# Hybrid FoX / RWKV-7 / retention decoder step: FoX q, k and v projections issued in thirds between the steps of four small stages

## The reference

```
h = rms_norm(x, ln_mix_g);  p = h @ w_in          # 1024 -> FoX q,k,v (512 each), 8 forget, RWKV 896, retention q,k,v,g (256 each)
FoX (8 heads of 64): q,k = rms_norm per head; logf = log_sigmoid(f + b); c = cumsum(logf)
     softmax(q k^T / 8 + c_i - c_j) v, causal; sample tokens also attend 8 cached pages of 128 rows
RWKV-7 (4 heads): S = S*w_t + (S a_t) b_t + v_t k_t; y = S r_t; head norm; bonus; gate
retention (4 heads): q,k = rotary; chunks of 128: o = ((q k^T) * dmask) v + (q R) * cross; R = R*gamma + k^T v; head norm; silu gate
x += [FoX | RWKV | retention] @ w_out
x += (silu(rms_norm(x) @ w_gate) * (rms_norm(x) @ w_up)) @ w_down          # width 2816
```

## Time and profile before

| | |
|---|---|
| median of 3 runs | 4695.26 us (4687.84 to 4697.62) |
| profiled execution | 4687.26 us; its span 4685.7 us, mean granted TensorE clock 0.922 |
| PE busy | 4225.7 us (90%) |
| DVE, ACT, POOL busy | 1385.4 (30%), 689.0 (15%), 344.1 (7%) |
| bytes moved | 249.85 MB, 53 GB/s over the span |

### The profile page before, as it was taken

One profiled execution on the slowest core, in us unless ns is written; L12 is line 12 of the kernel. 1 busy time (PEld: TensorE's weight loads), 2 busy tenths in 40 slices (PEclk: granted clock), 3 DMA queues, 4 the chain that ended last, 5 costly groups with the idle time before them and its releaser, 6 DMA issues.

```text
span 4685.7 us, 58583 instructions
## 1 busy us (share of the span) xinstructions
PE 4225.7 (90%) x21814; PEld 3157.0 (67%) x21814; DVE 1385.4 (30%) x2991; ACT 689.0 (15%) x1311; POOL 344.1 (7%) x590
## 2 busy tenths in 40 slices
PE   8888798978788999999998888889787989999998
PEld 5677576765456888866656775768454568888665
DVE  3444314034314333310043451230443143333001
ACT  2222101034200000000022220110442000000000
POOL 1000002211110000000010000021112000000000
PEclk9988795999899999999998897879997989999998
DMA  4300110112441111221123001001127211111212
GB/s 122 19 0 0 33 32 10 34 43 85 163 164 46 45 45 36 57 72 31 40 74 10 0 0 42 23 20 24 57 73 261 91 36 36 45 45 44 70 37 68
DMA packets 277943, 249.85 MB, mean 53 GB/s; under 512 B 24636, under 2 KB 237696, under 8 KB 276496
## 3 DMA queue, kind: packets, MB, share of 16 engines
q1 hardware_dynamic: 244400, 144.89, 12.3%
q0 software_dynamic: 33376, 102.70, 6.5%
HBM read 214.70 MB, written 32.83 MB: 53 GB/s over the span
## 4 chain that ended last, share of the span: by engine, by line
PE 84%; DVE 7%; issue 5%; ACT 2%; DMA 1%; DVEq 0%; POOLq 0%; POOL 0%; ACTq 0%; SPq 0%
PE ps L878 80%; PE ps L882 4%; DVE hT L2197 0%; ACT wd L2520 0%; DVE hT L1615 0%; ACT big L2492 0%; DVE big L1837 0%; DVE big L1845 0%; DMA wd<-in_state_rwkv 0%; DMA ring<-in_w_out 0%; DVE big L1809 0%; DVE big L1807 0%; DVE big L1798 0%; DVE big L1805 0%; DVE big L1803 0%
## 5 line engine op out<-in xcount | busy, mean ns | idle before, releaser
L878 PE MATMUL ps<-hT,ring 128*128 128x352 f32 (+1 forms) x3712 | 1063.9, 440 | 28.4 <-DMA ring<-in_w_out 12.3
L878 PEld LDWEIGHTS ps<-hT,ring 128*128 128x128 f32 x3712 | 713.4, 193 | 340.3 <-issue 27.7
L878 PE MATMUL ps<-big,wd 128*128 128x352 f32 (+3 forms) x2576 | 703.5, 432 | 10.9 <-DVE big L1807 7.2
L878 PEld LDWEIGHTS ps<-big,wd 128*128 128x128 f32 (+2 forms) x2576 | 457.5, 190 | 250.1 <-issue 15.8
L878 PE MATMUL ps<-xT,ring 128*128 128x264 f32 x1408 | 345.9, 389 | 13.4 <-DVE xT L2225 13.4
L878 PE MATMUL ps<-big 128*128 128x128 f32 (+5 forms) x1520 | 265.3, 347 | 51.7 <-POOL big L716 14.8
L878 PEld LDWEIGHTS ps<-xT,ring 128*128 128x128 f32 x1408 | 269.5, 192 | 60.7 <-DVE xT L2225 14.2
L878 PEld LDWEIGHTS ps<-big 128*128 128x128 f32 (+3 forms) x1520 | 214.2, 226 | 90.7 <-issue 21.9
L878 PE MATMUL ps<-ring,hT 128*128 128x128 f32 (+1 forms) x2304 | 261.5, 275 | 0.0
L878 PEld LDWEIGHTS ps<-ring,hT 128*128 128x128 f32 (+1 forms) x2304 | 256.9, 183 | 5.2 <-issue 2.4
L878 PE MATMUL ps<-hT,wd 128*128 128x264 f32 x1056 | 257.6, 387 | 0.0
(11 more groups left out here) (379 smaller groups left out, 3914.9 us busy)
## 6 DMA issues: line engine op xcount, KB each, us to landing
ring<-in_w_in SPq DMA_DIRECT2D x60, 512.0 KB, 3.8
ring<-in_w_gate SPq DMA_DIRECT2D x44, 512.0 KB, 4.0
ring<-in_w_up SPq DMA_DIRECT2D x44, 512.0 KB, 4.1
wd<-in_w_down SPq DMA_DIRECT2D x16, 1408.0 KB, 6.9
x_kept<-xT POOLq DMA_DIRECT2D x32, 528.0 KB, 3.5
xT<-x_kept POOLq DMA_DIRECT2D x32, 528.0 KB, 8.7
big<-in_cache_fox_k SPq DMA_DIRECT2D x64, 256.0 KB, 5.2
big<-in_cache_fox_k POOLq DMA_DIRECT2D x64, 256.0 KB, 5.2
```

The lines of the kernel that those rows point to most:

```text
L878: return pe.matmul(out, lhsT, rhs, start=start, stop=stop, skip_group_check=True)
```

## The change

The order of the jobs becomes RWKV 0 to 7, FoX q 8 to 11, retention 12 to 19, FoX k 20 to 23, FoX v 24 to 27. A job can now be issued in three parts (`job_third`: one column block of 352 each; `job_tm` with `part`: three row tiles each), and other work stands between the parts in PE's queue:

- the 12 thirds of q between the steps of RWKV sample. The steps' PSUM regions move to banks 0 to 4, q uses 5 to 7; X0 and Y are issued in turns over the two halves of the rows, and Y's part that doesn't need U comes ahead of the wait for it;
- the rotations of retention's q and k (now two blocks of 512, the 32 sample columns of all four tiles in one small matmul) between the thirds of retention's own jobs; DVE's passes are 1024 columns;
- the 12 thirds of k in retention: two around the first scores, one after each chunk (`RET_JOB`), two after the sample's sums. The chunk loops of PE, DVE, ACT and POOL are written out, the ninth scores go, each chunk's tiles are transposed and copied out one chunk later, and POOL only makes the decayed q, in place; matmuls read q, k and v where they lie;
- the 12 parts of v: one before the sample's last transposes, then one before each tile's sum of squares (8 tiles, 1024 columns, one after the other in two buffers) and three at the end.

The evacuations of q and k go by `fox_qk_evac` on DVE (even) or ACT (odd), at written places in those queues. q and k lie in `xT` (`fqk = xT`), so the copies `qtp`, `ktp` are gone; the first factor carries the minus sign. The attention takes v of pairs 0 and 1 from `fv`, of 2 and 3 from POOL's copies. POOL asks for the masks and the decay rows of pairs 0 and 1 before the loop of 64 loads, and for the store of v after it. Three quarters of the first set of key pages are asked for earlier, by SP after retention and by POOL before attention's first store.

```diff
-J_R, J_EQ, J_EV, J_FQ, J_FV, J_OUT, J_FF = 0, 8, 12, 16, 24, 28, 36
+J_R, J_FQ, J_EQ, J_EV, J_FK, J_FV, J_OUT, J_FF = 0, 8, 12, 16, 20, 24, 28, 36
...
-        fqk = region((big, 0), 8, NT)
-        fv = region((big, 8 * NT), NTT + 1, FW)
-        FB = 8 * NT + (NTT + 1) * FW
-        fsq = region((big, FB), 2, NT)
...
+                    RT_POOL.mark(pool.tensor_tensor(q, q, cross, ALU.mult), rt_pool, "qd")
...
+            def job_third(l, j, b, bank, freed):
+                if b == 0:
+                    pe.wait_ge(loaded[j % RING], l * (16 * JOBS // RING) + 16 * (j // RING + 1))
+                    pe.wait_ge(*evac_at(l, freed))
+                for k in range(KT):
+                    last = mm(ps[:, bank + b, 0:TB], ring[:, j % RING, k, :], hT[:, k, TB * b:TB * b + TB], k == 0, k == KT - 1)
+                if b == 2:
+                    last.then_inc(gemm_done, 1)
+            def fox_q_third(l, j, b):
+                job_third(l, j, b, 5, j - 1)
+            def fox_k_third(l, j, b):
+                job_third(l, j, b, 0, j - 1 if j > J_FK else j - 2)
+            def fm_third(l, j, b):
+                job_third(l, j, b, 3 * (j % 2), j - 2)
+            def job_tm(l, j, part):
+                if part == 0:
+                    pe.wait_ge(loaded[j % RING], l * (16 * JOBS // RING) + 16 * (j // RING + 1))
+                    pe.wait_ge(evac[j % 2], l * HALF + (j // 2 + 1))
+                for i in range(3 * part, 3 * part + 3):
                     n = P if i < NTT else NS
                     for k in range(KT):
                         last = mm(ps[0:n, 3 * (j % 2) + i // 4, P * (i % 4):P * (i % 4) + P], hT[:, k, P * i:P * i + n], ring[:, j % RING, k, :], k == 0, k == KT - 1)
...
+                fox_q_third(l, J_FQ, 0)
+                fox_q_third(l, J_FQ, 1)
...
+                fox_q_third(l, J_FQ, 2)
...
+                fox_q_third(l, J_FQ + 1, 2)
...
+                for m in range(2):
+                    o = [ps[SR, 4 - x, 256 * x + HD * m:256 * x + HD * m + HD] for x in range(2)]
+                    for b in range(DB):
+                        for x in range(2):
+                            mm(o[x], rex[half(x), m, b, :], sts[half(x), m, b, :], m == 0 and b == 0, False)
+                    for x in range(2):
+                        mm(o[x], smat[6][SR, pos(2 * m + x), :], vts(2 * m + x), False, False)
+                fox_q_third(l, J_FQ + 2, 0)
                 pe.wait_ge(*ac("U"))
...
+                for i in range(4):
+                    fm_third(l, J_EQ + i, 0)
+                    if i:
+                        rotated(i - 1)
+                    fm_third(l, J_EQ + i, 1)
+                    fm_third(l, J_EQ + i, 2)
+                job_tm(l, J_EV, 0)
+                rotated(3)
...
+                    if c < NTT - 1:
+                        ret_scores(c + 1)
...
+                    if c:
+                        pe.wait_ge(rt_dve, RT_DVE.at(it, "R1"))
+                        rows_turned(c - 1)
+                    fox_k_third(l, *RET_JOB[c])
...
+                rows_turned(NTT - 1)
+                fox_k_third(l, J_FV - 1, 1)
+                fox_k_third(l, J_FV - 1, 2)
+                pe.wait_ge(*evac_at(l, J_FV - 1))
+                job_tm(l, J_FV, 0)
...
+                def squares_summed(t):
+                    pe.wait_ge(fn_dve, FN_DVE.at(l, f"sq{t}"))
+                    if t:
+                        pe.wait_ge(fn_act, FN_ACT.at(l, f"ln{t - 1}"))
+                    else:
+                        pe.wait_ge(re_act, RE_ACT.at(l, "ro"))
+                    pe.sem_inc(passed, 1)
+                    for a in range(2):
+                        last = mm(ps[:, 6 + a, :], blk[:, :], fsq[:, t % 2, 512 * a:512 * a + 512])
+                    FN_PE.mark(last, fn_pe, f"ss{t}")
+                for n in range(1, 9):
+                    job_tm(l, J_FV + n // 3, n % 3)
+                    squares_summed(n - 1)
+                job_tm(l, J_FV + 3, 0)
+                pe.wait_ge(fn_dve, FN_DVE.at(l, "sqs"))
+                pe.wait_ge(fn_act, FN_ACT.at(l, "ln7"))
...
+                def fox_qk_evac(j, bank):
+                    n = j - J_FQ if j < J_EQ else j - J_FK + 4
+                    on((x_out, l * (32 * KT) + 16 * KT), (gemm_done, l * PJOBS + j + 1))
+                    v.tensor_copy(fqk[:, n, :].rearrange("p (a b) -> p a b", a=3), ps[:, bank:bank + 3, 0:TB]).then_inc(evac[0], 1)
...
+                    if c in (0, 6):
+                        fox_qk_evac(RET_JOB[c][0], 0)
...
+                    if c == 3:
+                        fox_qk_evac(RET_JOB[c][0], 0)
...
+                decay_row_pair(0)
+                decay_row_pair(1)
                 with pool.Fori(0, DB) as b:
                     for j in range(NPG):
                         page = pool.value_load(ptab[0:1, bass.ds(b * NPG + j, 1)], min_val=0, max_val=N_POOL - 1)
                         pool.dma_start(lfp[:, j, bass.ds(b * FH, FH)], I["cache_fox_logf"][bass.ds(l, 1), bass.ds(page, 1)].rearrange("a n p h -> p (a n h)")).then_inc(past_in, 16)
...
+                half("cache_fox_k", key_in, 0, 0, range(1, 4))
```

More of the change, by code:

```diff
@@ L820, in _ @@
                         pool.sem_inc(passed, 1)
-                        half("cache_fox_k", key_in, 0, 0, range(4))
                         half("cache_fox_k", key_in, 0, 1, range(2))
@@ L1254, in _, with ret_scores @@
+                for j in range(J_EV + 1, J_FK):
+                    for part in range(3):
+                        job_tm(l, j, part)
+                fox_k_third(l, J_FK, 0)
+                pe.wait_ge(*evac_at(l, J_EV + 3))
+                pe.wait_ge(re_dve, RE_DVE.at(l, "adds"))
                 pe.sem_inc(passed, 1)
-                def ret_scores(it):
+                def ret_scores(c):
                     RQ_PE.start()
-                    pe.wait_ge(rt_pool, RT_POOL.at(it, "k"))
+                    tk = slice(P * c, P * c + P)
@@ L1266, in ret_scores, with rows_turned @@
                     RQ_PE.mark(last, rq_pe, "kt")
-                ret_scores(l * (NTT + 1))
-                with pe.Fori(0, NTT) as c:
+                def rows_turned(c):
+                    for m in range(2):
+                        last = tr(ps[:, 7, P + P * m:2 * P + P * m], evg[:, c, EW + P * m:EW + P * m + P])
+                    last.then_inc(ret_rows, 1)
+                ret_scores(0)
+                fox_k_third(l, J_FK, 1)
+                for c in range(NTT):
                     it = l * NTT + c
-                    now = l * (NTT + 1) + c
+                    tk = slice(P * c, P * c + P)
@@ new lines, in _ @@
+                    for x in range(2):
+                        h = 2 * m + x
+                        mm(o[x], stts[SR, pos(h), :], evg[SR, NTT, HD * h:HD * h + HD], True, False)
+                    for b in range(DB):
+                        for x in range(2):
+                            last = mm(o[x], qex[half(x), m, b, :], rss[half(x), m, b, :], False, b == DB - 1)
+                RE_PE.mark(last, re_pe, "O")
+                for h in range(EH):
+                    last = mm(ps[half(h), 3 + h // 2, :], kds[SR, h, :], vexe[SR, h].rearrange("p b e -> p (b e)"))
@@ new lines, in _ @@
+                pe.sem_inc(passed, 1)
+                for m in range(2):
+                    last = tr(ps[:, 7, NS * m:NS * m + NS], yne[SR, P * m:P * m + P])
+                RE_PE.mark(last, re_pe, "ro")
+                FN_PE.start()
+                def squares_summed(t):
+                    pe.wait_ge(fn_dve, FN_DVE.at(l, f"sq{t}"))
+                    if t:
+                        pe.wait_ge(fn_act, FN_ACT.at(l, f"ln{t - 1}"))
+                    else:
+                        pe.wait_ge(re_act, RE_ACT.at(l, "ro"))
+                    pe.sem_inc(passed, 1)
+                    for a in range(2):
+                        last = mm(ps[:, 6 + a, :], blk[:, :], fsq[:, t % 2, 512 * a:512 * a + 512])
+                    FN_PE.mark(last, fn_pe, f"ss{t}")
@@ new lines, in _ @@
+                rows_s = ropet[:, 0:4 * NS].rearrange("p (i t) -> p i t", i=4)
+                on(dv("add3"))
+                for i in range(2):
+                    mk(v.scalar_tensor_tensor(rows_s[:, 2 * i:2 * i + 2, :], ps[:, 6, 2 * NS * i:2 * NS * i + 2 * NS].rearrange("p (i t) -> p i t", i=2), scales[i], trig(sin_t), ALU.mult, ALU.mult), f"tss{i}")
+                on(dv("tss1"))
+                mk(v.tensor_tensor(eqk[:, 0:4, T:NT], eqk[:, 0:4, T:NT], rows_s, ALU.add), "adds")
+                evac_tm(l, J_EV, evg, 0)
```

563 lines of the change are left out of this document (277 added, 286 removed).

## The result

The changed kernel takes 4441.9 us (median of 4 runs, 4438.6 to 4451.0), the kernel before 4691.6 us (4 runs, 4683.7 to 4697.6): a ratio of 0.9472, 95% interval 0.945 to 0.9494. The forecast was 4465 us, in a range of 4415 to 4530; the gain came out 23 us larger. The profiled execution has a span of 4437.8 us, 247.9 less than the one before.

What follows compares the result with a forecast made beforehand. TensorE bounds the kernel; only its idle and half-clock time can be won. Gains 37.0 + 11.1 + 47.8 + 31.9 - 14 - 1.0 = 112.8 us a layer, 225.6 in two, from 4687.3 to 4461.7, plus 3: 4465 us, range 4415 to 4530.

Steps and rivals of the forecast that it cites:

- RWKV sample: Stage with q's thirds: 36.82 us at half clock times 0.57 is 21.0, less 2.0, plus 1.5 waits; gain 37.0.
- the pairing: RWKV sample: X0 and Y sums in turns over the two row halves save 2.0 us (0 to 4.4).
- Clock, the mis-sized term: RWKV sample and retention with thirds: granted clock 0.93 over 187 us, so 14 us lost a layer.
- Retention's own work: Retention: 78.01 us at half clock, times 0.59, becomes 46.0 at full; 3.5 us of waits; gain 47.8.
- Rotary: Rotary stage: 7.3 us of matmuls and 0.8 of waits left of 19.2 us; gain 11.1.
- Norms: q/k norms with v's thirds: 15.6 us own work plus 1.8 waits; gain 31.9.
- POOL: POOL's late 64 small loads delay k's first store, needed by attention's second pair: 0 to 4 us, taken as 1.0.
- the sign that the prediction had called wrong: Second attention pair: POOL as releaser with more than 4 us would show the forecast wrong.
- 1 (clock at 2.4 GHz throughout): Mixed stretches: no 14 us clock loss and chains pair fully; 129 us gained a layer, 4430 us; chance 0.15.
- 2: Rival: clock falls in each sparse piece, 13 x 3 = 39 us a layer; 4512 us; chance 0.12.
- 4: Rival: RWKV sample, retention and their thirds all run at half clock; 39 us slower a layer, 4765; chance 0.03.
- 3: Rival: PE waits bare for the 12 jobs' PSUM evacuations, 20 us a layer; 4508 us; chance 0.07.

Runs made afterwards that it cites:

- the experiment: Changed kernel with the X0 and Y matmuls of RWKV sample issued head after head, not in turns: 4448.1 us, ratio 0.949.
- The grouped kernel: Changed kernel with each retention chunk's eight O matmuls in two groups (four of 128 rows, then four of 64) instead of in turns: 4394.9 us, ratio 0.9365.
- the first joined kernel: Changed kernel with retention's O in two groups and GpSimd's early page loads behind its first store of k: 4388.6 us, ratio 0.9363.

## Why the prediction was right, and where it was wrong

The direction and the mechanism held: idle and half clock under four stages, both covered by thirds. By its own prices, with no clock term, the four stretches of the table above were to take:

| stretch | forecast | measured |
|---|---|---|
| RWKV sample, 11 thirds of q | 53.5 + 19.0 + 1.5 = 74.0 | 70.0 |
| rotary, 2 thirds, projections | 9.7 + 123.8 + 7.3 + 0.8 = 141.6 | 138.9 |
| retention, 11 thirds of k | 53.5 + 46.0 + 3.5 = 103.0 | 103.0 |
| norms, v | 65.4 + 15.6 + 1.8 = 82.8 | 82.2 |
| clock, first and third | 14 | in the above |

That is 415.4 against 394.1. (The forecast's 408 takes off 7.8 us of warming up that the old stages' sums held.) Against 408 it came out 14 us better up to attention and 4 worse in it: the difference, twice, is 20 of the 23 us by which the forecast was too high. Nearly all terms but POOL's were on the careful side (retention's share of the clock was 1 short), so little of the fit is luck.

- *RWKV sample.* Own work was to be 21.0 less 2.0, and waits 1.5. It was 70.0 - 53.5 = 16.5, with no wait. So the sum was 4.0 too high: 1.5 for waits, 0.4 for the pairing (2.4 by the experiment), and 2 for the factor 0.57 (16.5 + 2.4 is 0.51 of the 36.82). That the thirds cover the 6.04 and 7.64 us was right. That they are needed for the first of the two was wrong: q's work ahead of the steps covers it even in one piece.
- *Clock, the mis-sized term.* 14 us over both mixed stretches, of which 79/187, 6 us, lay in RWKV sample. There the clock was 1.00, so none was lost. In retention, whose share was 8, it fell in six of eight chunks. Own work at the full clock there is 8 chunks of 4.3 us (O 2.8, then 0.4, 0.6 and 0.5) and 5.7 for the sample's part and the first scores, 40.3. A third is 4.74 us there, from its start to the next operation's (713.38 to 718.12), 52.1 for eleven; with the wait of 1.3 that is 93.7, so 9 of the 103.0 are the clock. The grouped kernel says the same from the other side (9). So the term was 14 and the measured loss 9, all of it in retention. The argument against the Trainium skill's rule, from the earlier trace rows, was right: the clock fell with PE never idle. What I didn't see is what the falls hung on. I named "small alternating matmuls" and left their order as given; the order cost 10 us a layer itself, and without it the falls went too.
- *Retention's own work.* 46.0 was forecast at 0.59, and 40.3 it was. Three things make up the 5.7: a chunk is about 4.3 us against 7.8 at half, 0.55 and not 0.59 (2.5 in eight chunks); the sample's matmuls go in turns over heads too (799.78 to 804.62, 4.8 us, where before it was 12.3, which is 7.2 at 0.59), which the diff shows and the sum left out (2.4); and the ninth scores, which the prediction knew to go, stayed in its sum (1.9 at half, about 1). With waits of 1.3 in place of 3.5, the stage was 8.1 better than its forecast with clock.
- *Rotary.* Gain 13.8 in place of 11.1: no wait is left of the 0.8, and three of the projections' thirds between two rotations take 14.2 us (598.99 to 613.19) where I had 14.6.
- *Norms.* 16.8 against 17.4, right. But my reason for it, waits of 5 us covered by v, was only part: undone, the stage is 30.8, not 46. The other 15 us I put down to the wider sums and their chain; no run undoes those.
- *POOL.* 1.0 forecast (0 to 4), 6 measured. The issue of the first store was put at 45 us into attention and was 46.8; landing at 4 to 8 us was 4.8. The need was the fault. I read it from the earlier trace rows, 48.7 us in, a pair with its cold start. Without that cold start the second pair begins 45.8 us in, and the wait at half clock behind it costs a second time: 2.25 us of waiting became 6 us of pair. This is the sign that the prediction had called wrong, POOL as releaser in the second pair with more than 4 us, and it came: ScalarE waited 5.94 us for it. Attention so took 1.8 us more where 3.2 less 1.0 were to be won.
- *Rivals.* 1 (clock at 2.4 GHz throughout) was right for three stretches of four, and its 4430 is nearer than my 4465: 12 us off against 23 (the rivals' totals leave out the 3 us that I added to the forecast; with them it is 10). 2 was right in that the clock fell in most of retention's chunks, six of eight, but a fall cost 1.5 us, not 3, and none came in RWKV sample. 4 is refuted by the granted clock, 3 by the one wait of 1.3 us.

What carried the gain of 127.3 us a layer up to attention, by the experiments' stages: placing the thirds between the steps 24 (q: 98.7 us with twelve thirds in one piece, against 74.9), about 30 (k: 137.8 against 108.0) and 14 (v: 96.5 against 82.2), 68 in all; the rest is from whole jobs standing ahead of the stages and from copies and narrow sums taken out, and wasn't tried one by one. The medians give 62 for the three, with the second pair's 6 in v's.

## What to carry to other kernels

Fill thin stages with pieces of dense work, but look first at the thin work's own order: matmuls of 128 and of 64 rows in turns cost 2.8 us where two groups cost 1.5, and between retention's dense thirds the clock fell only with the turns. Price a filler by undoing it alone: here the three placements were worth 24, 30 and 14 us where their stages' forecast gains were 37.0, 47.8 and 31.9, because the rest of the change (whole jobs ahead of the stage, wider sums, shorter chains) must have given the other part; it was not undone piece by piece. And when a stage gets shorter, walk every queue that was asleep beside it (GpSimd's 92 us of small loads) and read the time of need from a warm stage, not from the cold one of the old trace.

## What the runs showed of the hardware

- The granted clock falls from 1.00 to 0.50, of 2.4 to 1.2 GHz, while PE is busy without a gap (741.6 to 744.6), and stays at 1.00 with the same chunk 1.3 us leaner. Halving the groups of small matmuls left falls in four of eight chunks; without dense work between, it is 0.51 and 0.52 for the whole stage, whatever O's order.
- Matmuls of 64 columns that change between 128 and 64 rows start 0.36 us apart at the full clock and 0.62 at half. Grouped, they start 0.23 (128 rows) and 0.15 us (64 rows) apart at full; the row half in which the 64 lie made no difference (0.67 and 0.66 us for four).
- At a head pair's start the clock is at 1.00 in some pairs and 0.50 in others of the same kernel (transposes of 1.09 and 1.97 us). A pair that keeps 1.00 takes 43.6 us, one with half clock in part of its first 12 us 45.2 to 46.4: 1.6 to 2.8 us, more than some of the edits are worth. A start at 1.00 doesn't ensure it: the second pair of the first joined kernel starts so and takes 45.2, with 0.86 over its first 12.4 us.
